# Six of eight GLU projection chunks as seven block products, with convolution steps moved to later stages, in a one-core decoder layer

## The chip, the cores and the metric

The kernel runs on one core of one Trainium2 chip. The metric is the device time of one execution in microseconds (us). Engines are named as in the profile: PE (TensorE, matmuls), PEld (its weight loads), DVE (VectorE), ACT (ScalarE), POOL (GpSimd), SP (SyncE, which here only issues transfers). PEq, ACTq, POOLq and SPq are the queues of instructions that issue DMAs.

## The reference, cut to what matters

One decoder layer for 512 prompt tokens and 8 sample tokens (520 rows together), width 1024:

```
xn   = rmsnorm(x);  proj = xn @ w_in
a_b, a_c, a_x, b_val, b_glu, q, gate_logits = split(proj)
ya = (a_b * dwconv3(a_c * a_x)) @ w_out_a
ub = b_val * sigmoid(b_glu)                                  # the GLU
yb = silu(layernorm(dwconv31(ub) + bias)) @ w_out_b          # 31 taps, depthwise, causal
yx = softmax(q k^T / 16) v @ w_out_x
h  = x + (g0 * ya + g1 * yb + g2 * yx) @ w_o;  h = h + SwiGLU(rmsnorm(h));  rmsnorm(h)
```

The change touches how `b_val` and `b_glu` (each 1024 columns of `xn @ w_in`) are multiplied, and when the 31 taps of `dwconv31` are computed. Outputs stay those of the reference.

## The kernel before

**Tiling.** Activations lie transposed: 8 tiles of 128 channels by 520 tokens (`TOK`; `HALF` is 260). A projection is done in chunks of 256 output columns over all 1024 input channels: a chunk is 1 MB of weights and two output tiles of 128 channels, each of which takes both 1 KB halves of one PSUM buffer (`acc`, four of them, used in turn; `free(use)` makes PE wait until the use four back was read, through the counter `acc_read`).

**Precision.** Each float32 operand is split in a high part (rounded by an ACT copy) and a low part (difference). A product is high x high + high x low + low x high: for a chunk 2 tiles x 8 input tiles x 2 halves x 3 = 96 matmuls of 128x128 by 260 columns, 64 with the high weights and 32 with the low (`chunk`, L2218 and L2236).

**Weights.** SP loads a chunk into one of two raw slots; ACT makes the high part (`hi_part`, L749) and mostly a negated copy (`negative`, L752), onto which POOL issues an accumulating DMA that adds the raw weights, which leaves the low part (L727; PE waits on `w_rest`). For the chunks listed in `SUB` (chunk 9, the second of the GLU stage, is the last before the convolution stages) POOL subtracts itself, two TENSOR_TENSOR of 128x1024 (L723).

**Stages**, in PE's order: keys and values; GLU (chunks 8 to 15: even chunks give gates, odd ones values; two chunks are a pair); queries and attention (Q, four heads); the products of the width-3 convolution (CX); branch X (gate and output chunks in turns, four pairs, on DVE in a loop of two); BA; branch A (four pairs); layer norm, branch B; w_o; feed-forward (FFN). All engines have one fixed order, written out by hand. DVE fills time between its stage duties with taps of the width-31 convolution: `conv` (L1462), 8 tiles x 32 steps (31 taps and one small step for the samples), each step dependent on the last. Before the change 62 steps lie in the GLU stage, 34 in Q, 32 in CX, 64 in X, 32 in BA and 32 in A.

**Seven block products.** Most FFN chunks already go as one level of Strassen-Winograd over 2x2 blocks: the 1024x256 weights and the 1024x520 activations are each cut in four, seven products of 512x128 by 512x260 replace eight, each of 12 matmuls, so 84 in place of 96 (`seven`, L2544 and L2551). DVE must make four sums of weight blocks, their low parts, and combine the products (7 adds of 260 columns); ACT makes the high parts and copies the first product out of PSUM after the third.

**Opening and end of the GLU stage.** DVE's last work before it is L1437 and L1441 (clearing of the convolution's padding); its first product of gates and values comes at the end of the first pair (L1487, which reads PSUM and frees it). ACT loads keys of the sample group (`load_k`, 1 MB each) in this stage, and splits the first Q chunk at its end.

Of the kernel before, what the change touches and what calls it, by code (L numbers as in the profile page):

```python
# [58 lines left out]
PARTS = ((0, 4), (4, 6), (10, 4), (14, 8))  # L59
PAIRS = HK  # L60
SEVEN = 8


def ffn_order():
# [150 lines left out]
def decoder_step(nc, x_prompt, x_sample, mem_prompt, cache_mem_k, cache_mem_v, state_conv_a,  # L215
# [109 lines left out]
    ln_sum = at("ln_sum", [P, TOK], f32, o_p2l)  # L325
    uao = at("uao", [TS + 2, D], f32, o_p2h)

    hg = [at(f"hg_{n}", [P, KT, TOK], f32r, o_ub + 4 * ACTV * i) for i, n in enumerate("hl")]
    y_st = at("y_st", [P, 4, D], f32, o_xh)
    ys_st = at("ys_st", [TS, D], f32, o_xh + 16 * D)  # L330
# [57 lines left out]
    with ctx:  # L388
# [38 lines left out]
        state_sum = sem("state_sum")  # L427
        pads = sem("pads")
        b_sig = sem("b_sig")
        ubo_stored = sem("ubo_stored")  # L430
        q_hi = sem("q_hi")
        q_rep = sem("q_rep")
# [130 lines left out]
        def ob(n):  # L563
            return T[f"ob{n // 2}"] + n % 2

        z_tmp = [ubyb[:, KT, 0:TOK], sg[:, 0, 0:TOK]]

        def kept(c, rows):
# [15 lines left out]
        def _(sp):  # L584
            def load(c, slot, src, col, k0=0, kn=KT):

                if not isinstance(c, int):
                    sp.wait_ge(w_own, own(c) - 4)
                elif c - 2 >= OWN:
                    sp.wait_ge(w_own, own(c - 2))  # L590
                elif c - 2 in SUB:
                    sp.wait_ge(w_sub, subtracted(c - 2))
                elif c >= 2:
                    sp.wait_ge(w_rest[slot], turn(c - 2) * 16)
                sp.dma_start(w_raw[:, slot, 0:kn, :], src[:, k0:k0 + kn, bass.ds(col, CW)]) \
                    .then_inc(w_loaded[slot], 16)

# [99 lines left out]
        def _(pool):  # L697
# [14 lines left out]
            for c in range(1, OWN):  # L712
                if c in SUB:
                    if c == 1:
                        pool.wait_ge(refined, 5)
                    if 2 <= c < C_B + 2:
                        pool.wait_ge(acc_done, T[f"kv{c - 2}"] + 1)
                    elif c >= C_B + 2:
                        pool.wait_ge(acc_done, T["c1" if c == C_CX + 2 else f"cx{c - C_CX - 2}"] + (1 if c == C_CX + 2 else 2))
                    for s in range(2):  # L720
                        ks = slice(s * HK, (s + 1) * HK)
                        pool.wait_ge(w_hi, 2 * c + s + 1)
                        nc.gpsimd.tensor_tensor(w_l[:, c % 2, ks, :], w_raw[:, c % 2, ks, :], f(w_h[:, c % 2, ks, :]),  # L723
                                                ALU.subtract).then_inc(w_sub, 1)
                else:
                    pool.wait_ge(w_neg, sum(n not in SUB for n in range(c + 1)))
                    pool.dma_start(w_l[:, c % 2, :, :].rearrange("p k n -> p (k n)"),  # L727
                                   w_raw[:, c % 2, :, :].rearrange("p k n -> p (k n)"),
                                   accum_op=ALU.add).then_inc(w_rest[c % 2], 16)
# [11 lines left out]
        def _(act):  # L741
# [138 lines left out]
            act.wait_ge(x_kept, 16 * 5)  # L880


            for p in range(4):
                u0 = T["b"] + 4 * p
                split(C_B + 2 * p + 1, 1, u0 - 1)
                for j in range(2):
                    done(u0 + j)

                    act.wait_ge(acc_read, u0)
                    nc.scalar.activation(two(sg[:, j, 2:SG]), halves(u0 + j), ACT.Sigmoid).then_inc(b_sig, 1)  # L890
# [365 lines left out]
        def _(dve):  # L1256
# [206 lines left out]
                    ins.then_inc(cv_step, 1)  # L1463

            CV = K_B + 1
            Q4 = (range(0, 12), range(12, 16), range(16, 28), range(28, CV))

            dve.wait_ge(pads, 1)  # L1470
            for i in range(2):
                for p in range(2):
                    u0 = T["b"] + 8 * i + 4 * p
                    if i + p:
                        dve.wait_ge(acc_read, T["b"] + 4)
                    if i == 0 and p == 1:
                        conv(0, range(20))
                    elif i and p == 0:
                        conv(0, range(20, K_B))
                        conv(1, range(9))  # L1480
                    elif i:
                        conv(1, range(9, 29))
                    dve.wait_ge(b_sig, 4 * i + 2 * p + 2)
                    for j in range(2):
                        n = 4 * i + 2 * p + j
                        done(u0 + 2 + j)
                        V.tensor_tensor(two(ubyb[:, n + 1, PAD:SLOT]), halves(u0 + 2 + j), two(sg[:, j, 2:SG]),  # L1487
                                        ALU.mult).then_inc(acc_read, 1 if j else 3)

            conv(1, range(29, K_B))  # L1490


            dve.wait_ge(acc_read, T["b"] + 16)
# [62 lines left out]
            taps = (0, 14, 19, 24, 29)  # L1556
            for h in range(NH):
                if h == 0:
                    conv(2, range(0, 3))
                q_lo(h, 0)  # L1560
                if h:
                    probs_lo(h - 1)
                conv(2, range(taps[h], taps[h] + 3) if h else range(3, 8))
                q_lo(h, 1)
                if h == 0:
                    done(T["btail"])
                    V.tensor_copy(ubo[:, :].rearrange("p (b c) -> p b c", b=2),
                                  acc[T["btail"] % 4][0:PAD + TS, :, :]).then_inc(acc_read, 1)
                    conv(0, [K_B])
                    conv(1, [K_B])  # L1570
# [5 lines left out]
                conv(2, range(taps[h] + 3, taps[h + 1]) if h else range(8, 11))  # L1576
                normalise(h, 1)
                if h:
                    sample_scores(h - 1, 1)
                if h == 0:  # L1580
                    conv(2, range(11, taps[1]))
            dve.wait_ge(c_copied, 1)
            probs_lo(3, 2)
            sample_scores(3, 0)
# [6 lines left out]
            conv(2, range(taps[NH], CV - 1))  # L1591

            conv(2, [K_B])

            def group_max():

# [65 lines left out]
            for it in range(4):  # L1662
# [11 lines left out]
                    group_max()  # L1674
                if it == 3:
                    sample_lo(0)
                conv(3, C3[it][0])
# [5 lines left out]
                for j in range(2):  # L1683
# [13 lines left out]
                conv(3, C3[it][1])  # L1697
                if it < 2:
                    sample_sum(it)
            sample_norm(2)  # L1700
# [1 line left out]
            sample_norm(3)  # L1702
            sample_lo(2)
            sample_lo(3)
            conv(3, range(24, CV))


            with dve.Fori(0, 2) as i:
                for p in range(2):
                    u0 = i * 8 + (T["x"] + 4 * p)  # L1710
                    conv(i + 4, Q4[2 * p])
                    dve.wait_ge(x_sig, i * 4 + (2 * p + 2))
                    for j in range(2):
                        done(u0 + (2 + j))
                        dst = merged_f[:, bass.ds(i * (4 * TOK) + (2 * p + j) * TOK, TOK)]
                        V.tensor_tensor(two(dst), halves(T["x"] + 4 * p + 2 + j), two(sg[:, j, 2:SG]),
                                        ALU.mult).then_inc(acc_read, 1 if j else 3)
                        if j == 0:
                            conv(i + 4, Q4[2 * p + 1])


            def ba_lo_part(n):
# [16 lines left out]

            dve.wait_ge(cs_step, KT - 1)  # L1740
            dve.wait_ge(cv_step, (KT - 1) * K_B)
            for k in range(1, KT - 1):
                V.tensor_tensor(ln_sum[:, :], ubyb[:, k, 0:TOK], ubyb[:, 0, 0:TOK] if k == 1 else ln_sum[:, :],
                                ALU.add).then_inc(ln_step, 1)
                dve.wait_ge(ln_step, k)


            for it in range(4):
                u0 = T["a"] + 4 * it
                if it < 3:  # L1750
                    conv(KT - 1, (range(0, 11), range(11, 22), range(22, CV))[it])
                else:
                    dve.wait_ge(cs_step, KT)
                    dve.wait_ge(cv_step, KT * K_B)
# [425 lines left out]
        def _(pe):  # L2180
# [195 lines left out]
            def q_tile(h, j):  # L2376
# [345 lines left out]
```

## Time and profile before

| | |
|---|---|
| Median of 3 runs | 1069.52 us (1069.45 to 1069.84) |
| The profiled execution's own time | 1069.33 us |
| Its span, first to last instruction | 1067.6 us (1.7 us of its time lie around the span) |
| Mean granted TensorE clock | 0.997 of full |
| DVE, ACT, POOL busy | 718.2, 479.7, 110.8 us |
| DMA, mean | 175 GB/s |

In timelines a row is: start in us from the span's start, duration in us, engine, line, operation, output<-inputs, shape, count, and in brackets the idle time before it with what ended it. A matmul's recorded duration (0.28 us) overlaps those of its neighbours; the distance between starts is what counts. Some matmul records can be missing.

### The profile page before, as it was taken

Reading aid. Unit: us, or ns where it says so; the run is one execution under the profiler, and the core shown is the slowest. Engines: PE = TensorE matmul, PEld = TensorE weight load, DVE = VectorE, ACT = ScalarE, POOL = GpSimd, SP = SyncE. Lnnn points to the kernel's source line nnn. Section 1 sums busy time; section 2 is a strip of 40 time slices with the busy share of each in tenths; the row PEclk is TensorE's granted clock in tenths of the full one; section 3 lists DMA queues with packets and bytes.
Section 4 is the critical chain, followed back from the end, with each engine's and each line's share of the span. In section 5 each row is a group of like instructions: output and inputs, shape, how many; then the busy total and the mean of one; then the engine's idle time right before and its main releaser. Section 6 shows DMA issues by size and latency. Waiting matters only on the chain.

```text
span 1067.6 us, 20526 instructions
## 1 busy us (share of the span) xinstructions
PE 1057.3 (99%) x8751; PEld 1051.1 (98%) x8751; DVE 718.2 (67%) x1234; ACT 479.7 (45%) x550; POOL 110.8 (10%) x93
## 2 busy tenths in 40 slices
PE   9999999999999999999999999999999999999997
PEld 9999999999999999999999999999999999999996
DVE  6766677888888654686323755578778457588754
ACT  6744443453335353344345723344456245366431
POOL 3661000002300000000000000000000000000000
PEclk9999999999999999999999999999999999999998
DMA  8967886689796878758876663231578365487512
GB/s 293 289 189 190 222 208 154 195 228 316 215 274 140 208 172 195 177 148 192 207 187 158 160 237 116 81 99 40 152 185 198 114 148 145 119 199 176 169 41 80
DMA packets 151194, 187.25 MB, mean 175 GB/s; under 512 B 4759, under 2 KB 141295, under 8 KB 145591
## 3 DMA queue, kind: packets, MB, share of 16 engines
q1 hardware_dynamic: 117734, 106.64, 31.8%
q0 software_dynamic: 8496, 57.15, 26.7%
q10 hardware_dynamic: 24880, 22.26, 6.9%
q8 instruction: 63, 1.03, 0.4%
q14 instruction: 21, 0.16, 0.1%
HBM read 122.34 MB, written 7.54 MB: 122 GB/s over the span
## 4 chain that ended last, share of the span: by engine, by line
PE 96%; DVE 3%; ACT 0%; issue 0%; POOL 0%; DVEq 0%; POOLq 0%
PE acc L2218 39%; PE acc L2236 20%; PE acc L2592 12%; PE acc L2544 11%; PE acc L2551 6%; PE acc L2329 2%; PE acc L2190 2%; PE acc L2337 1%; PE acc L2433 1%; PE acc L2409 1%; DVE o_acc L1631 0%; DVE ubyb L1462 0%; DVE yA L1693 0%; PE acc L2494 0%; DVE w_l L1337 0%
## 5 line engine op out<-in xcount | busy, mean ns | idle before, releaser
L2218 PE MATMUL acc<-big_h,w_h 128*128 128x260 f32 x1664 | 337.2, 284 | 0.1
L2218 PE MATMUL acc<-big_l,w_h 128*128 128x260 f32 x1664 | 334.4, 282 | 0.0
L2218 PEld LDWEIGHTS acc<-big_h,w_h 128*128 128x128 f32 x1664 | 255.8, 188 | 0.7 <-DVE st L1667 0.3
L2218 PEld LDWEIGHTS acc<-big_l,w_h 128*128 128x128 f32 x1664 | 256.4, 189 | 0.0
L2236 PE MATMUL acc<-big_h,w_l 128*128 128x260 f32 x1664 | 209.0, 283 | 0.0
L2236 PEld LDWEIGHTS acc<-big_h,w_l 128*128 128x128 f32 x1664 | 203.7, 189 | 0.1
L1462 DVE SCALAR_TENSOR_TENSOR ubyb<-ubyb,prm 128x512 f32<-128x512 f32 (+1 forms) x240 | 180.3, 751 | 15.1 <-DVE ubyb L1462 9.4
L749 ACT ACTIVATE w_h<-w_raw 128x1024 fp32r<-128x1024 f32 x120 | 120.2, 1051 | 103.5 <-DMA w_raw<-in_w_out_a_dram 29.7
L2544 PE MATMUL acc<-x_h,ws_h 128*128 128x260 f32 x504 | 126.0, 282 | 0.0
L2544 PE MATMUL acc<-x_l,ws_h 128*128 128x260 f32 x504 | 125.8, 282 | 0.0
L2544 PEld LDWEIGHTS acc<-x_h,ws_h 128*128 128x128 f32 x504 | 94.9, 188 | 0.2
L2544 PEld LDWEIGHTS acc<-x_l,ws_h 128*128 128x128 f32 x504 | 94.9, 188 | 0.0
L752 ACT ACTIVATE w_l<-w_raw 128x2048 fp32r<-128x2048 f32 x41 | 78.2, 1908 | 12.7 <-PE acc L2236 12.7
L727 POOL DMA_DIRECT2D w_l<-w_raw x41 | 35.1, 856 | 464.6 <-ACT w_l L752 464.6
L2551 PE MATMUL acc<-x_h,ws_l 128*128 128x260 f32 x504 | 81.2, 283 | 0.0
L2592 PE MATMUL acc<-mid,wd_h 128*128 128x260 f32 x576 | 72.6, 283 | 0.0
L2592 PEld LDWEIGHTS acc<-mid,wd_h 128*128 128x128 f32 x576 | 70.6, 189 | 0.0
L2551 PEld LDWEIGHTS acc<-x_h,ws_l 128*128 128x128 f32 x504 | 69.0, 188 | 0.0
L723 POOL TENSOR_TENSOR w_l<-w_raw,w_h 128x1024 fp32r<-128x1024 f32 x22 | 59.1, 2712 | 45.6 <-ACT w_h L749 32.3
L733 POOL DMA_DIRECT2D ws_l<-w_raw x18 | 15.3, 848 | 368.3 <-ACT ws_l L1168 368.3
L1168 ACT ACTIVATE ws_l<-w_raw 128x1536 fp32r<-128x1536 f32 x18 | 26.8, 1491 | 57.4 <-PE acc L2551 23.0
L1976 DVE TENSOR_TENSOR ws_f<-w_raw 128x1024 f32<-128x1024 f32 x18 | 22.0, 1223 | 32.9 <-PE acc L2592 15.9
(278 smaller groups left out, 1327.8 us busy)
## 6 DMA issues: line engine op xcount, KB each, us to landing
w_l<-w_raw POOLq DMA_DIRECT2D x41, 1024.0 KB, 8.1
w_raw<-in_w_in_dram SPq DMA_DIRECT2D x36, 1024.0 KB, 5.3
ws_l<-w_raw POOLq DMA_DIRECT2D x18, 768.0 KB, 7.4
w_raw<-in_w_ff_gate_dram SPq DMA_DIRECT2D x18, 512.0 KB, 5.0
w_raw<-in_w_ff_up_dram SPq DMA_DIRECT2D x18, 512.0 KB, 4.9
k_st<-in_cache_mem_k_dram ACTq DMA_DIRECT2D x8, 1024.0 KB, 8.2
v_st<-in_cache_mem_v_dram ACTq DMA_DIRECT2D x8, 1024.0 KB, 12.6
w_raw<-in_w_v_dram SPq DMA_DIRECT2D x4, 1024.0 KB, 8.0
```

What stands on the lines that cost most here:

```text
L723: nc.gpsimd.tensor_tensor(w_l[:, c % 2, ks, :], w_raw[:, c % 2, ks, :], f(w_h[:, c % 2, ks, :]), ALU.subtract).then_inc(w_sub, 1)
L727: pool.dma_start(w_l[:, c % 2, :, :].rearrange("p k n -> p (k n)"), w_raw[:, c % 2, :, :].rearrange("p k n -> p (k n)"), accum_op=ALU.add) ...
L749: nc.scalar.activation(w_h[:, slot, ks, :], w_raw[:, slot, ks, :], ACT.Copy).then_inc(w_hi, 1)
L752: nc.scalar.activation(w_l[:, slot, :, :], w_raw[:, slot, :, :], ACT.Copy, scale=-1.0).then_inc(w_neg, 1)
L1168: nc.scalar.activation(ws_l[s % 2][:, 0:3, :, :].rearrange("p b r n -> p (b r n)"), raw_f[:, s % 2, 1:4, :].rearrange("p b n -> p (b n)"), ...
L1462: ins = V.scalar_tensor_tensor(y, u, w, y, ALU.mult, ALU.add)
L1976: V.tensor_tensor(x[:, 3:5, :], raw_f[:, s % 2, 0:1, :].broadcast_to([P, 2, PAIRS * P]), raw_f[:, s % 2, 1:3, :], ALU.add).then_inc(st_sum, 1)
L2218: last = M.matmul(out[:, b, 0:HALF], w_h[:, slot, k, cols], xs[:, k_at + k, b * HALF:(b + 1) * HALF], start=start and k == 0 and xs is x[0 ...
L2236: last = M.matmul(out[:, b, 0:HALF], w_l[:, slot, k, cols], x[0][:, k_at + k, b * HALF:(b + 1) * HALF], start=False, stop=stop and k == ks ...
L2544: M.matmul(out, ws_h[slot][:, w, r, :], x_part[:, r, x, :], start=r == 0 and x_part is x_h, stop=False)
L2551: last = M.matmul(out, ws_l[slot][:, w, r, :], x_h[:, r, x, :], start=False, stop=r == PAIRS - 1)
L2592: last = M.matmul(out[:, b, 0:e - a], w, inner(kind[1], k, a, e), start=begin and k == ks[0] and kind is kinds[0], stop=end and k == ks[-1 ...
```

## The change

Chunks 10 to 15 of the GLU stage (`GLU_SEVEN = range(2, 8)`, j = 2 to 7) are computed by `glu_seven`, 84 matmuls each, in the same order of products as in the FFN. For them the weights are loaded as two DMAs of 512-byte rows; POOL's accumulating DMA covers three of four blocks. The four block combinations of `xn` are made once, by DVE (`xn_f` = high + low part again, then t1 to t4, then their low parts) and ACT (high parts), while PE does chunks 0 and 1. Results are left in quarters of `sg` (gates) and `ubyb` (values), which also hold the first product and its sums. The first `load_k` pair moves behind the split of the second Q chunk, as the region is now in use. Convolution steps per stage become 15 (GLU), 32 (Q), 32 (CX), 92 (X, unrolled), 40 (BA), 45 (A); the sum over the first seven tiles for the layer norm moves behind the first 13 steps of A. The core of the diff:

```diff
+GLU_SEVEN = range(2, 8)
@@ sync, load()
+                if isinstance(c, int) and c - C_B in GLU_SEVEN:
+                    for half, b, landed_ in ((1, 0, w_half), (0, 2, w_loaded)):
+                        sp.dma_start(raw_f[:, slot, b:b + 2, :]..., src[:, :, col + half * P:...]).then_inc(landed_[slot], 16)
+                    return
@@ scalar
-            for p in range(4):
-                split(C_B + 2 * p + 1, 1, u0 - 1)
-                for j in range(2): ... Sigmoid
-                split(C_B + 2 * p + 2, 0, u0 + 1)
-                if p >= 2:
-                    load_k(0, p - 2)
+            split(C_B + 1, 1, T["b"] - 1)
+            for n in range(4):
+                turned_hi(n)
+            for j in range(1, 8):
+                n, e = j + 1, j - 1
+                if j == 1:
+                    for i in range(2):
+                        done(T["b"] + i)
+                        nc.scalar.activation(two(sg[:, i, 2:SG]), halves(T["b"] + i), ACT.Sigmoid).then_inc(b_sig, 1)
+                if n < 8:
+                    glu_negative(n)
+                if j >= 2:
+                    glu_copy(j)          # waits for the third product of chunk j
+                if n < 8:
+                    glu_hi_sums(n, 0)
+                    glu_hi_sums(n, 1)
+                    glu_hi_raw(n)
+                else:
+                    split(C_Q, 0, T["b"] + 13)
+                if e % 2 == 0 and e:
+                    act.wait_ge(acc_read, T["b"] + 2 * e + 2)
+                    nc.scalar.activation(sg[:, :, 2:SG], sg[:, :, 2:SG], ACT.Sigmoid).then_inc(b_sig, 1)
...
+                if h == 0:
+                    for u in range(2):
+                        load_k(0, u)
@@ vector
+            a_, b_ = xn_f[:, 0:PAIRS, :], xn_f[:, PAIRS:KT, :]
+            dve.wait_ge(nrm_lo, 5)
+            for ks in (slice(0, PAIRS), slice(PAIRS, KT)):
+                V.tensor_tensor(xn_f[:, ks, :], f(xn[0][:, ks, :]), f(xn[1][:, ks, :]), ALU.add).then_inc(t_step, 1)
+            ...
+            V.tensor_tensor(t1, a_[:, :, early], a_[:, :, late], ALU.subtract).then_inc(t_step, 1)
+            V.tensor_tensor(t2, b_[:, :, late], t1, ALU.add).then_inc(t_step, 1)
+            V.tensor_tensor(t3, a_[:, :, late], b_[:, :, late], ALU.subtract).then_inc(t_step, 1)
+            V.tensor_tensor(t4, b_[:, :, early], t2, ALU.subtract).then_inc(t_step, 1)
...
+            for n in range(4):
+                turned_lo(n)
+            for j in range(1, 8):
+                n, e = j + 1, j - 1
+                if e == 1:
+                    dve.wait_ge(b_sig, 2)
+                    for i in range(2):
+                        done(T["b"] + 2 + i)
+                        V.tensor_tensor(two(ubyb[:, i + 1, PAD:SLOT]), halves(T["b"] + 2 + i), two(sg[:, i, 2:SG]),
+                                        ALU.mult).then_inc(acc_read, 1 if i else 3)
+                elif e > 1:
+                    glu_combine(e)       # five adds of 260 columns
+                    if e % 2:
+                        glu_product(e)
+                if n < 8:
+                    glu_sums(n, 0)
+                if j >= 2:
+                    glu_first(j)         # two adds of 260, behind glu_copy
+                if n < 8:
+                    glu_sums(n, 1)
+                    glu_low(n, 0)
+                    glu_low(n, 1)
+                if j >= 2:
+                    taps((2, 2, 0, 2, 0, 7)[j - 2])
+            glu_combine(7)
+            glu_product(7)
+            taps(2)
...
-            with dve.Fori(0, 2) as i:
-                for p in range(2):
-                    conv(i + 4, Q4[2 * p]) ... product ... conv(i + 4, Q4[2 * p + 1]) ... product
+            for p in range(4):
+                taps(17)
+                dve.wait_ge(x_sig, 2 * p + 2)
+                for j in range(2):
+                    done(u0 + 2 + j)
+                    V.tensor_tensor(two(merged[:, 2 * p + j, :]), ..., ALU.mult).then_inc(acc_read, 1 if j else 3)
+                    if j == 0:
+                        taps(6)
...
-                conv(6, range(4 * n, 4 * n + 4))
+                taps(5)
...
+                    else:
+                        taps((KT - 1) * CV - made)
+                        sum_first_tiles()
@@ tensor
+            def glu_seven(j):
+                free(u)
+                free(u + 1)
+                for n, (out, w, x) in enumerate(((Y, s1, t1), (X, s2, t2), (P_, a11, b11), (Z, a22, t4), (P_, a12, b21),
+                                                 (X, s3, t3), (Y, s4, b22))):
+                    ...      # waits: b_hi, b_lo (n < 2); w_hi, w_rest (n == 2); b_copy (4); b_uv (5, 6)
             for j in range(8):
-                chunk(C_B + j, j % 2, T["b"] + 2 * j, T["b"] + 2 * j, xn)
+                if j not in GLU_SEVEN:
+                    chunk(C_B + j, j % 2, T["b"] + 2 * j, T["b"] + 2 * j, xn)
+                    continue
+                if j == GLU_SEVEN[0]:
+                    pe.wait_ge(t_lo, 4)
+                glu_seven(j)
```

## Rows read from the trace of the kernel before

**Rows 1.** The page, part 1: busy us, share of the span, instructions.
```profile
PE 1057.3 (99%) x8751; PEld 1051.1 (98%) x8751; DVE 718.2 (67%) x1234; ACT 479.7 (45%) x550; POOL 110.8 (10%) x93
```

**Rows 2.** Waits of PE, whole span, longest first: us, times, longest.
```profile
PE acc L2190 <- POOL ident L703: 1.6, 1, 1.6
```

**Rows 3.** Timeline of DVE, GLU stage: second products of two pairs.
```profile
89.14 0.70 DVE L1487 TENSOR_TENSOR ubyb<-acc,sg 128x520 f32<-128x520 f32 x1 [1.11 <-PE acc L2236]
...
112.12 0.70 DVE L1487 TENSOR_TENSOR ubyb<-acc,sg 128x520 f32<-128x520 f32 x1 [1.11 <-PE acc L2236]
```

**Rows 4.** Timeline of DVE, FFN: first work behind two successive seven-product chunks.
```profile
829.13 0.43 DVE L2010 TENSOR_TENSOR cp<-acc,cp 128x260 f32<-128x260 f32 x1 [2.16 <-PE acc L2551]
...
839.17 0.43 DVE L2010 TENSOR_TENSOR cp<-acc,cp 128x260 f32<-128x260 f32 x1 [0.39 <-PE acc L2551]
```

**Rows 5.** Groups of DVE instructions in the FFN: count, busy us, mean ns, idle before.
```profile
L1988 DVE TENSOR_TENSOR ws_l<-ws_f,ws_h 128x1024 fp32r<-128x1024 f32 x36 | 42.3, 1217 | 0.0
L1979 DVE TENSOR_TENSOR ws_f<-ws_f,w_raw 128x512 f32<-128x512 f32 x18 | 12.5, 693 | 0.6
L2025 DVE TENSOR_TENSOR up_f<-up_f,gs 128x1040 f32<-128x1040 f32 x9 | 11.1, 1233 | 0.1
```

**Rows 6.** Timeline of DVE, before the GLU stage and in CX.
```profile
57.54 2.79 DVE L1313 TENSOR_TENSOR big_l<-nrm_o,big_h 128x1024 fp32r<-128x1024 f32 x1
...
71.93 0.26 DVE L1441 MEMSET ubyb<- 128x240 f32 x1
...
267.58 5.63 DVE L1631 SCALAR_TENSOR_TENSOR o_acc<-v_st,pT,o_acc 128x256 f32<-128x256 f32 x14
```

**Rows 7.** Timeline of PE: start of the third GLU chunk.
```profile
88.93 0.40 PE L2218 MATMUL acc<-big_h,w_h 128*128 128x260 f32 x2
```

**Rows 8.** Timeline of POOL, GLU stage and CX.
```profile
72.91 4.74 POOL L723 TENSOR_TENSOR w_l<-w_raw,w_h 128x1024 fp32r<-128x1024 f32 x2 [5.10 <-ACT w_h L749]
...
105.22 0.84 POOL L727 DMA_DIRECT2D w_l<-w_raw  x1 [13.00 <-ACT w_l L752]
...
151.20 0.84 POOL L727 DMA_DIRECT2D w_l<-w_raw  x1 [13.03 <-ACT w_l L752]
...
269.59 8.41 POOL L723 TENSOR_TENSOR w_l<-w_raw,w_h 128x1024 fp32r<-128x1024 f32 x2 [6.46 <-ACT w_h L749]
```

**Rows 9.** Timeline of SP: weight loads that waited for those POOL transfers.
```profile
112.19 0.37 SPq L595 DMA_DIRECT2D w_raw<-in_w_in_dram  x1
...
160.34 12.66 SPq L595 DMA_DIRECT2D w_raw<-in_w_in_dram  x2
```

**Rows 10.** Timeline of ACT: the split of the first Q chunk.
```profile
147.10 2.00 ACT L749 ACTIVATE w_h<-w_raw 128x1024 fp32r<-128x1024 f32 x2
149.00 1.91 ACT L752 ACTIVATE w_l<-w_raw 128x2048 fp32r<-128x2048 f32 x1
```

**Rows 11.** Timeline of DVE: end of CX, and branch X.
```profile
332.44 5.47 DVE L1462 SCALAR_TENSOR_TENSOR ubyb<-ubyb,prm 128x512 f32<-128x512 f32 x7
...
371.88 0.70 DVE L1716 TENSOR_TENSOR merged<-acc,sg 128x520 f32 x1 [7.04 <-PE acc L2236]
```

**Rows 12.** Timeline of DVE: end of BA, start of branch A.
```profile
472.29 1.20 DVE L1736 COPY uao<-acc 10x1024 f32<-10x1024 f32 x1
...
474.13 3.64 DVE L1743 TENSOR_TENSOR ln_sum<-ubyb,ln_sum 128x520 f32<-128x520 f32 x5
...
487.83 0.70 DVE L1760 TENSOR_TENSOR sg<-acc,sg 128x520 f32<-128x520 f32 x1 [1.59 <-PE acc L2236]
488.64 0.70 DVE L1763 TENSOR_TENSOR merged<-merged,sg 128x520 f32<-128x520 f32 x1
```

**Rows 13.** Window at the end: length, busy PE, PEld, DVE, ACT, POOL, PEclk, DMA, GB/s.
```profile
1060.00:1064.00 4.00, 0.65 (x8) 0.54 (x8) 3.45 (x11) 1.54 (x3) 0.00 (x0) 0.72 0.12 46
```

**Rows 14.** Timeline of PE, first microseconds of the span.
```profile
1.59 3.67 PE L2190 MATMUL acc<-ident 128*128 128x128 f32 x16 [1.59 <-POOL ident L703]
...
8.40 0.82 PE L2190 MATMUL acc<-ident 128*128 128x128 f32 x6
```

More of the change, by code:

```diff
@@ L880, in _, with turned_hi @@
             act.wait_ge(x_kept, 16 * 5)
-            for p in range(4):
-                u0 = T["b"] + 4 * p
-                split(C_B + 2 * p + 1, 1, u0 - 1)
[L886 to L890, printed above, removed]
-                split(C_B + 2 * p + 2, 0, u0 + 1)
-                if p >= 2:
-                    load_k(0, p - 2)
+            def turned_hi(n):
+                act.wait_ge(t_step, 2 + n + 1)
+                nc.scalar.activation(tx[0][:, n, :, :].rearrange("p r t -> p (r t)"), tx_f[:, n, :], ACT.Copy).then_inc(t_hi, 1)
@@ new lines, in glu_first, with combs @@
+            def glu_first(j):
+                u, k = T["b"] + 2 * j, j - 2
+                m1, v, u2, _ = glu_quarters(j)
+                dve.wait_ge(b_copy, k + 1)
+                V.tensor_tensor(u2, m1, acc[u % 4][:, 1, 0:HALF], ALU.subtract).then_inc(b_uv, 1)
+                dve.wait_ge(b_uv, 2 * k + 1)
+                V.tensor_tensor(v, acc[(u + 1) % 4][:, 0, 0:HALF], u2, ALU.add).then_inc(b_uv, 1)
+            def combs(j):
+                return sum(5 if n % 2 else 4 for n in range(2, j))
@@ new lines, in glu_combine @@
+            def glu_combine(j):
+                u, k = T["b"] + 2 * j, j - 2
+                c11, c12, c21, c22 = glu_quarters(j)
+                P_, X, Y, Z = (acc[(u + n // 2) % 4][:, n % 2, 0:HALF] for n in range(4))
+                dve.wait_ge(b_uv, 2 * k + 2)
+                done(u + 1)
+                V.tensor_tensor(c22, X, c12, ALU.subtract).then_inc(b_comb, 1)
+                V.tensor_tensor(c21, X, c21, ALU.subtract).then_inc(b_comb, 1)
+                V.tensor_tensor(c11, P_, c11, ALU.add).then_inc(b_comb, 1)
+                dve.wait_ge(b_comb, combs(j) + 1)
+                V.tensor_tensor(c12, Y, c12, ALU.add).then_inc(b_comb, 1)
+                dve.wait_ge(b_comb, combs(j) + 2)
+                ins = V.tensor_tensor(c21, Z, c21, ALU.add)
+                ins.then_inc(*((b_comb, 1) if j % 2 else (acc_read, 2)))
@@ L1562, in _ @@
                     probs_lo(h - 1)
-                conv(2, range(taps[h], taps[h] + 3) if h else range(3, 8))
+                taps(3 if h else 5)
                 q_lo(h, 1)
@@ L1575, in _ @@
                 query_rows(h)
-                conv(2, range(taps[h] + 3, taps[h + 1]) if h else range(8, 11))
+                taps(q_taps[h + 1] - q_taps[h] - 3 if h else 3)
                 normalise(h, 1)
@@ L1580, in _ @@
                 if h == 0:
-                    conv(2, range(11, taps[1]))
+                    taps(3)
             dve.wait_ge(c_copied, 1)
@@ L1696, in _ @@
                         group_bias()
-                conv(3, C3[it][1])
+                taps(len(C3[it][1]))
                 if it < 2:
@@ L1704, in _ @@
             sample_lo(3)
-            conv(3, range(24, CV))
-            with dve.Fori(0, 2) as i:
[L1709 to L1719, printed above, removed]
+            taps(8)
+            for p in range(4):
+                u0 = T["x"] + 4 * p
+                taps(17)
+                dve.wait_ge(x_sig, 2 * p + 2)
+                for j in range(2):
+                    done(u0 + 2 + j)
+                    V.tensor_tensor(two(merged[:, 2 * p + j, :]), halves(u0 + 2 + j), two(sg[:, j, 2:SG]),
+                                    ALU.mult).then_inc(acc_read, 1 if j else 3)
+                    if j == 0:
+                        taps(6)
             def ba_lo_part(n):
@@ L1737, in _, with sum_first_tiles @@
                 .then_inc(acc_read, 1)
[L1740 to L1745, printed above, removed]
+            def sum_first_tiles():
+                dve.wait_ge(cs_step, KT - 1)
+                dve.wait_ge(cv_step, (KT - 1) * K_B)
+                for k in range(1, KT - 1):
+                    V.tensor_tensor(ln_sum[:, :], ubyb[:, k, 0:TOK], ubyb[:, 0, 0:TOK] if k == 1 else ln_sum[:, :],
+                                    ALU.add).then_inc(ln_step, 1)
+                    dve.wait_ge(ln_step, k)
             for it in range(4):
@@ L1750, in _ @@
                 if it < 3:
-                    conv(KT - 1, (range(0, 11), range(11, 22), range(22, CV))[it])
+                    if it:
+                        taps((KT * CV - made) // (3 - it))
+                    else:
+                        taps((KT - 1) * CV - made)
+                        sum_first_tiles()
                 else:
```

164 lines of the change are left out of this document (139 added, 25 removed).

## The prediction, made before the result was known

> **What bounds the kernel now.** I read the page's busy times first, then PE's waits, then the timelines of the GLU stage engine by engine, then the same of the FFN, where the new kind of chunk already runs. The page has PE busy 99% of the span [rows 1], and its longest wait in the whole span is 1.6 us, before any data is there [rows 2]; no other is over 0.5. So PE sets the time everywhere, and no stage has slack that would take up a new stall: a matmul saved is time saved, and a microsecond in which PE waits is a microsecond lost. The reader is to see both sides of that in what follows.
>
> **What PE saves.** The second products of two pairs lie 22.98 us apart, each with the same short wait for PE [rows 3], so a plain chunk takes 11.49 us for its 96 matmuls. Two successive seven-product chunks in the FFN end 10.04 us apart [rows 4], 84 matmuls at the same 0.120 us. The difference is 1.45 us, times six chunks: -8.7 us.
>
> **Inside the six chunks** I replayed DVE's and ACT's lists from the start S of a chunk. DVE on an odd j: combine from S+0.2 (five adds of 260 columns, 0.43 each by [rows 4], 0.34 apart where pipelined: 1.7), first weight sums 1.2, a wait for ACT's copy of the third product (3 x 12 x 0.120 = 4.3, done by S+4.9), two adds, to S+5.8, two sums of 512 (1.4), two low parts (2.4) [rows 5], two taps: free at S+11.0, 0.8 behind the next chunk's first duty. On an even j the product of gates and values (1.23, the 1040-element row of [rows 5]) takes the place of the taps: free at S+9.7 of a chunk of 10.04, so the lag is gone. PE's nearest demand, the second add before its seventh product, stands at S+8.6 against S+6.0. ACT ends at S+10.6 at worst. I put stalls here at 0; the bound above is the 0.8 lag at each of three pairs, 2.4 us.
>
> **The opening** is where cover is missing. PE may start chunk 10 only when DVE's product of the first pair has freed PSUM (`free`), and the new order puts that product behind everything DVE makes for the block products. DVE is free at 72.2, after the clearing of the padding [rows 6]. Its list: two sums of 2080 elements (1.233 us at 1040 against 0.693 at 512 is 1.02 ns an element [rows 5], so 2.3 each, 4.55), four of 1040 (4.8), their four low parts (4.65), the three weight sums (1.2 + 0.7 + 0.7), two low parts of 1024 (2.35), the product itself (0.70, [rows 3]). Sum 19.7: 91.9. PE wants chunk 10 at 88.9 [rows 7]. That alone is a stall of 3.0.
>
> It is not alone. POOL's two subtractions for chunk 9 start at 72.91 and take 4.74 us [rows 8] while DVE is idle in the kernel before; now they fall on top of DVE's sums. A DVE instruction of two SBUF operands, 1024 elements, took 2.79 us at 57.54, while POOL ran the same kind of subtraction [rows 6], against 1.22 for that size in the FFN [rows 5]: they take turns, and the one waits for the other's whole instruction. DVE's new list has such instructions one upon the other, so both subtractions are inserted whole: +4.75, DVE reaches 96.6, and the opening stall is 7.7. ACT's four high parts, table load, sigmoids and the negation end near 91.2 and POOL's transfer lands by 98.7, before PE wants it at 100.4; they hide. From below the collision costs nothing, if POOL is the one held off.
>
> The Trainium skill (SBUF — State Buffer, on engine ports) says that DVE with two SBUF inputs and a GpSimd instruction that reads SBUF exclude each other, and that whoever issues first wins. DVE's first sum, at 72.2, is first. By the trace this can go on: at 269.59 two subtractions took 8.41 us, as DVE's 14 back-to-back instructions at 0.40 us each lost nothing meanwhile [rows 6, 8]. By that reading DVE would lose nothing until a gap; but five of the new instructions wait for the one before, and a gap is all that POOL needs, so I stay with 4.75.
>
> **The clock.** A PE idle for 7.7 us may come back slower. In the last 4 us with matmuls the granted clock averages 0.72 [rows 13]: between its two levels, 2.4 and 1.2 GHz (1.00 and 0.50), that is 1.8 us at the upper, though PE was busy for 0.65 us only; it fell about 1.1 us after the last matmul. In the opening 16 transposes took 3.67 us, 0.23 each, and 6 later ones 0.82, 0.11 apart [rows 14]: half speed for about 5.4 us after the first matmul. If that recurs, 5.4 us at half speed lose 2.4 to 2.7; I take 2.5, from 0 to 2.7. The skill (TensorE: Matmul & The Clock Gate, Part 1) agrees in kind: throttled is the default, and activity lifts it.
>
> **The end of the GLU stage.** The first Q chunk's split now stands behind ACT's copy in chunk 15: with S7 the start of that chunk, copy to S7+4.8, two high parts 2.0, negation 1.9 [rows 10], POOL's transfer at S7+8.9. From POOL's issue to the load that waits for its landing is 7.0 us where no other transfer runs (105.22 to 112.19) and 9.1 where one of the key loads does (151.20 to 160.34) [rows 8, 9]. The key loads are now issued at about S7+13.7, so I take 7.0 and a little: landing at S7+16.0. PE asks for that low part 32 matmuls into the first Q tile, at S7+10.04+3.83 = 13.9. Stall 2.2 (2.0 to 4.1 by the two rows). Before, the landing was at 160.3 against a demand at 161.7.
>
> **The moved steps.** A tap is 0.785 us (7 in 5.47, [rows 11]). 47 fewer in the GLU stage pay for the new sums. In X each pair gets 17 + 6. Inside the stage DVE needs 23 x 0.785 + 1.4 = 19.5 of 22.98 us and keeps up, the more so as the unrolled steps lose some 0.15 us each of loop arithmetic. But at its start DVE comes straight from CX: 8 steps from 332.4, then 16 and the small one, ends at 351.5. The product is due at 371.88 - 22.98 = 348.9 [rows 11] and frees the PSUM that PE needs 1.6 us later, at 350.5 (at 88.93 PE began the next chunk [rows 7], and the first product of that pair had begun 1.11 + 0.70 ahead of 89.14 [rows 3], at 87.3); it now frees it at 352.25. Stall 1.75 (0 to 2.6).
> BA: 5 taps and two operations of 520 elements (0.70 each) are at most 5.35 of the 48 x 0.120 = 5.75 us of a tile; it keeps up, but ends later: the copy at 472.29 [rows 12] moves to 474.4, two more taps and the exchange of a small step for a tap. Then 12 taps and a small step (9.7), and only then the 4.3 us of sums that used to come first (473.5 to 477.8): 489.7, where the first product of A is due at 487.83 and was released with its merge at 489.34, just ahead of PE [rows 12]. Stall 1.7 (0 to 2.2). In CX the exchange of a small step for a tap costs at most 0.1.
>
> **The sum**, against the profiled execution: 1069.33 - 8.7 + 7.7 + 2.5 + 2.2 + 1.75 + 1.7 + 0.1 = 1076.6, which stands 7.1 us above the median before, 0.7%. The profiled execution is 0.2 below the median of the runs shown, which is nothing beside this. Other edits are taken at nothing: the two half loads of 512-byte rows (the FFN's chunks have the same and keep 10.04), the keys, which land during the first head and are read in the second, and the unrolled loop.
>
> **The rivals.**
> R1, no slower clock: everything else as above, 1074.1. For it: that the clock fell so soon at the end may be due to the thin work ahead of it, and here PE comes out of a dense stretch. Against: 7.7 us is long beside 1.1.
> R2, no collision with POOL: DVE goes on undisturbed, the opening stall is 3.0 and the clock holds: 1069.33 - 8.7 + 3.0 + 5.75 = 1069.4, no change. For it: the 14 undelayed instructions. Against: the 2.79 us one, and there are others of 2.3 to 2.9 like it.
> R3, the other side: the opening list fits. It decides at the product's place: if DVE's sums of 2080 elements and POOL's turns together cost no more than lets the product end by 88.9 to 89.7 (a list of 17 us or less, not 24.4), the first stall vanishes, and 1069.33 - 8.7 + 5.75 = 1066.4; with the X and A stalls gone as well 1062.9. For it: each of these durations is read from another place. Against: it needs 3 us less than the sum without any collision.
> R4, the chunks don't keep their 10.04: DVE's lag isn't worked off (for a collision with POOL's descriptor work, say), 2.4 us or more on top: 1079 and up.
>
> **How the numbers follow.** The forecast 0.42, R1 0.22, R2 0.10, R3 0.10, R4 0.16. A measurement of this kernel can tell about 0.2%, 2.1 us, from no change. Forecast, R1 and R4 are slower beyond that, 0.78 with small parts of R1 lost to no change; R2 falls within; R3 is faster. So slower 0.78, same 0.11, faster 0.11. For 8 in 10 I leave out R3 and the tail of R4: 1069.2 to 1080.5; the likeliest case by itself spans 1074.5 to 1078.5.
>
> **What would show it.** In the trace after: PE idle 7 to 8 us before the third GLU chunk, near 96.6, released by DVE's product; DVE's sums of 2080 and 1040 elements and POOL's subtractions stretched, 4.7 us between them; a granted clock below 1 right after; then six chunk ends 10.04 apart; a wait of PE on the w_l transfer of 2 us in the first Q tile; waits on DVE of 1.5 to 2 us at the second gate chunk of X and of A. It is wrong if PE starts chunk 10 before 93, if the chunks are further apart than 10.1, or if the total of PE's new waits is under 10 us.

## The result, and the profile after

The changed kernel takes 1087.11 us (median of 4, 1083.71 to 1087.76) beside 1069.68 for the one before in the same session (4, 1069.45 to 1070.41): a ratio of 1.0155 (ratios here and below are of the means), 95% interval 1.0134 to 1.0177; by the medians it is 17.4 us slower. The forecast was 1076.6, slower by 7.1, and its range ended at 1080.5. The profiled executions are 1087.76 and 1069.33, the spans 1086.0 and 1067.6. The ledger below goes by the spans, +18.4.

The page after (busy us, share of the span, instructions), beside [rows 1]: 72 matmuls fewer, PE's busy time 1.6 us less, and yet the span is longer: PE now stands still, where it did not before. DVE has 64 us more work.

```profile
PE 1055.7 (97%) x8679; PEld 1048.3 (97%) x8679; DVE 782.1 (72%) x1313; ACT 491.8 (45%) x563; POOL 111.1 (10%) x93
```

PE's waits after, by whom they were for, beside [rows 2] (us in total, times, longest). The largest total stands on a transfer, not on DVE:

```profile
PE acc L2432 <- DMA w_l<-w_raw: 8.2, 2, 4.7
PE acc L2600 <- DVE ubyb L1666: 7.9, 1, 7.9
PE acc L2414 <- DVE merged L1906: 1.6, 1, 1.6
PE acc L2386 <- POOL ident L746: 1.6, 1, 1.6
PE acc L2790 <- ACT cp L1284: 1.0, 2, 0.6
```

DVE's timeline after, in the opening (start, us, instruction), where [rows 6] had only the clearing of the padding. Two sums of 2080 elements took 6.76 us together (2.33 and 4.52 one by one, overlapping by 0.1), the next two, of 1040, took 3.33 and 1.24; the product, two halves, is the last but one line:

```profile
73.11 0.26 DVE L1537 MEMSET ubyb<- 128x240 f32 x1
73.41 6.76 DVE L1577 TENSOR_TENSOR xn_f<-big_h,big_l 128x2080 f32<-128x2080 f32 x2
80.20 3.33 DVE L1580 TENSOR_TENSOR tx_f<-xn_f 128x1040 f32<-128x1040 f32 x1
83.57 1.24 DVE L1582 TENSOR_TENSOR tx_f<-xn_f,tx_f 128x1040 f32<-128x1040 f32 x1
...
96.76 1.30 DVE L1666 TENSOR_TENSOR ubyb<-acc,sg 128x520 f32<-128x520 f32 x2
97.98 1.22 DVE L1604 TENSOR_TENSOR sw_f<-w_raw 128x1024 f32<-128x1024 f32 x1
```

POOL's timeline after, which answers to [rows 8]: its two subtractions took 8.34 us (3.90 and 4.48 one by one) for 4.74. The last two lines are the transfers of which the waits below speak.

```profile
74.09 8.34 POOL L766 TENSOR_TENSOR w_l<-w_raw,w_h 128x1024 fp32r<-128x1024 f32 x2 [3.96 <-ACT w_h L797]
...
159.66 0.84 POOL L775 DMA_DIRECT2D w_l<-w_raw  x1 [15.92 <-ACT w_l L800]
...
492.96 0.86 POOL L775 DMA_DIRECT2D w_l<-w_raw  x1 [18.03 <-ACT w_l L800]
```

PE's timeline after at the three long waits; the second line, the start of chunk 10, answers to [rows 7]. The matmuls beside each wait are the measure of the clock: 16 with the low part took 3.84 us at 169.53 and 2.09 at 177.93, 32 took 5.61 at 501.42 and 4.00 at 85.79.

```profile
85.79 4.00 PE L2432 MATMUL acc<-big_h,w_l 128*128 128x260 f32 x32
97.72 0.56 PE L2600 MATMUL acc<-tx_h,sw_h 128*128 128x260 f32 x1 [7.92 <-DVE ubyb L1666]
...
169.53 3.84 PE L2432 MATMUL acc<-big_h,w_l 128*128 128x260 f32 x16 [4.72 <-DMA w_l<-w_raw]
...
177.93 2.09 PE L2432 MATMUL acc<-big_h,w_l 128*128 128x260 f32 x16
...
501.42 5.61 PE L2432 MATMUL acc<-big_h,w_l 128*128 128x260 f32 x32 [3.48 <-DMA w_l<-w_raw]
```

Windows after around them (the clock is the third number from the end): 2.4 GHz before the first wait, 1.2 GHz behind all three. In the first and second the clock fell while PE still waited. In the third it fell about 1.5 us after PE had started again: that was at 501.42, and the window to 503 still has 0.98.

```profile
85.00:89.00 4.00, 4.00 (x36) 4.00 (x35) 3.96 (x4) 3.83 (x4) 0.00 (x0) 1.00 0.66 178
89.00:95.00 6.00, 0.79 (x7) 0.59 (x5) 5.90 (x7) 4.59 (x6) 1.00 (x1) 0.86 0.25 49
95.00:100.00 5.00, 2.29 (x10) 2.32 (x11) 4.20 (x5) 3.27 (x3) 0.86 (x1) 0.50 0.61 126
169.00:175.00 6.00, 5.47 (x25) 5.47 (x26) 0.89 (x3) 0.60 (x1) 0.00 (x0) 0.50 1.07 256
501.00:503.00 2.00, 1.58 (x13) 1.58 (x14) 0.87 (x2) 0.00 (x0) 0.00 (x0) 0.98 1.05 201
503.00:506.00 3.00, 3.00 (x15) 3.00 (x15) 1.40 (x2) 0.00 (x0) 0.00 (x0) 0.50 0.85 136
```

And ACT's copies of the third product of the seven-product chunks; the first and the last of six are 50.33 us apart, 10.07 each:

```profile
104.94 0.39 ACT L962 ACTIVATE sg<-acc 128x260 f32<-128x260 f32 x1 [6.67 <-PE acc L2608]
115.00 0.39 ACT L962 ACTIVATE ubyb<-acc 128x260 f32<-128x260 f32 x1 [2.74 <-PE acc L2608]
...
155.27 0.39 ACT L962 ACTIVATE ubyb<-acc 128x260 f32<-128x260 f32 x1 [4.84 <-PE acc L2608]
```

**The ledger of the spans** (waits by their brackets). PE comes to the opening 0.7 us later than before: its 32 matmuls with the low part of chunk 9 start at 85.79 for 85.10, ahead of all that was changed. The six chunks give back 8.5. The opening stall costs 7.9 and the clock behind it 2.7: the first 36 matmuls of chunk 10 took 7.0 us, where 0.120 each make 4.3. The first Q tile costs 4.7, and its clock 2.6: from 169.53 on, 26 matmuls took 5.76 us where 0.120 each make 3.12. X costs 1.6. A costs 3.5, and its clock 1.6 in 32 matmuls. In the FFN, PE waits 1.0 us for ACT's copy. The sum is 17.8. The other 0.6 is in the waits: counted between the starts of matmuls, each is 0.1 to 0.2 us longer than in its bracket.

### The profile page after: what moved, and what is told of

Same layout as the page of the kernel before. It is cut to its first block, busy times and chain, and to the rows that moved or that the text cites. A ratio compares the mean times of both kernels' runs of the same rounds, so it can differ in the third digit from the quotient of the medians.

```text
span 1086.0 us, 20360 instructions
## 1 busy us (share of the span) xinstructions
PE 1055.7 (97%) x8679; PEld 1048.3 (97%) x8679; DVE 782.1 (72%) x1313; ACT 491.8 (45%) x563; POOL 111.1 (10%) x93
## 4 chain that ended last, share of the span: by engine, by line
PE 59%; DVE 4%; DMA 4%; ACT 1%; issue 0%; ACTq 0%; SPq 0%; DVEq 0%
PE acc L2414 23%; PE acc L2432 12%; PE acc L2838 11%; PE acc L2790 9%; PE acc L2797 5%; DVE ubyb L1558 2%; DMA ws_l<-w_raw 1%; DMA w_raw<-in_w_ff_gate_dram 1%; DMA w_raw<-in_w_ff_up_dram 1%; DMA w_l<-w_raw 1%; PE acc L2386 0%; ACT ws_l L1264 0%; PE acc L2740 0%; DVE ws_f L2172 0%; ACT ws_h L1272 0%
## 5 line engine op out<-in xcount | busy, mean ns | idle before, releaser
L2414 PE MATMUL acc<-big_h,w_h 128*128 128x260 f32 x1472 | 298.5, 284 | 1.7 <-DVE merged L1906 1.6
L2414 PE MATMUL acc<-big_l,w_h 128*128 128x260 f32 x1472 | 296.1, 283 | 0.0
L2414 PEld LDWEIGHTS acc<-big_h,w_h 128*128 128x128 f32 x1472 | 227.0, 189 | 2.5 <-issue 1.8
L2414 PEld LDWEIGHTS acc<-big_l,w_h 128*128 128x128 f32 x1472 | 227.1, 189 | 0.0
L2432 PE MATMUL acc<-big_h,w_l 128*128 128x260 f32 x1472 | 188.2, 285 | 8.2 <-DMA w_l<-w_raw 8.2
L2432 PEld LDWEIGHTS acc<-big_h,w_l 128*128 128x128 f32 x1472 | 183.3, 191 | 8.6 <-DMA w_l<-w_raw 8.6
L1558 DVE SCALAR_TENSOR_TENSOR ubyb<-ubyb,prm 128x512 f32<-128x512 f32 x240 | 180.3, 751 | 7.3
L797 ACT ACTIVATE w_h<-w_raw 128x1024 fp32r<-128x1024 f32 x108 | 108.2, 1052 | 90.0 <-DMA w_raw<-in_w_in_dram 24.7
L775 POOL DMA_DIRECT2D w_l<-w_raw x35 | 29.9, 855 | 422.7 <-ACT w_l L800 422.7
L800 ACT ACTIVATE w_l<-w_raw 128x2048 fp32r<-128x2048 f32 x35 | 66.8, 1908 | 8.6 <-PE acc L2432 8.6
```

The costliest lines, as they stand in the source:

```text
L797: nc.scalar.activation(w_h[:, slot, ks, :], w_raw[:, slot, ks, :], ACT.Copy).then_inc(w_hi, 1)
L800: nc.scalar.activation(w_l[:, slot, :, :], w_raw[:, slot, :, :], ACT.Copy, scale=-1.0).then_inc(w_neg, 1)
L1558: ins = V.scalar_tensor_tensor(y, u, w, y, ALU.mult, ALU.add)
L2414: last = M.matmul(out[:, b, 0:HALF], w_h[:, slot, k, cols], xs[:, k_at + k, b * HALF:(b + 1) * HALF], start=start and k == 0 and xs is x[0 ...
L2432: last = M.matmul(out[:, b, 0:HALF], w_l[:, slot, k, cols], x[0][:, k_at + k, b * HALF:(b + 1) * HALF], start=False, stop=stop and k == ks ...
```

## The experiments

Four kernels on one chip, beside 1070.34 us for the kernel before (7 runs); then three on another, beside 1071.09 (15 runs). The kernel before was thus 0.7 and 1.4 us slower there than in the session above, by whose times the expectations go.

**Without the collision in the opening.** Chunk 9's low part comes from ACT's negation and POOL's transfer; the subtraction is gone.

```
-SUB = (*range(C_B + 2), C_CX + 2, C_CX + 4)
+SUB = (*range(C_B + 1), C_CX + 2, C_CX + 4)
```

> The changed kernel, with the low part of chunk 9 made by ACT's negated copy and an accumulating transfer, so that GpSimd subtracts nothing in the opening of the GLU stage. Theory (collision plus clock): DVE's two sums of 2080 elements take 2.3 us each again, its list ends 4.7 us earlier, the wait of PE before the third chunk falls from 7.9 to about 3.2 us, and the clock stays at its upper level there, which gives back another 2.8: 7.5 us less than the changed kernel, about 1079.5. Rival (DVE's list is long by itself, GpSimd only fills gaps in it): the wait stays at 7 or more and the time at 1087. A third way, the collision goes but the clock falls all the same: 4.7 less, 1082.4.

Measured: 1081.02 us (1078.06 to 1082.84), 1.0097 of before (1.0071 to 1.0123). Its DVE timeline has the undisturbed durations, and its PE timeline a wait of 3.05 us:

```profile
71.92 4.56 DVE L1577 TENSOR_TENSOR xn_f<-big_h,big_l 128x2080 f32<-128x2080 f32 x2
76.52 1.24 DVE L1580 TENSOR_TENSOR tx_f<-xn_f 128x1040 f32<-128x1040 f32 x1
```

```profile
91.94 0.36 PE L2600 MATMUL acc<-tx_h,sw_h 128*128 128x260 f32 x1 [3.05 <-DVE ubyb L1666]
...
92.97 0.74 PE L2608 MATMUL acc<-tx_h,sw_l 128*128 128x260 f32 x4
...
95.25 1.07 PE L2608 MATMUL acc<-tx_h,sw_l 128*128 128x260 f32 x4
...
97.39 0.64 PE L2608 MATMUL acc<-big_h,w_l 128*128 128x260 f32 x4
```

The collision was worth 2.2 + 2.1 us in two instructions, 4.3 where 4.75 was forecast. The stall fell by 4.9; the other 0.6 is that DVE began its list 1.5 us earlier than after, and PE came to the stall only 0.9 earlier. The clock fell all the same, after 1.5 us of matmuls at full speed: four took 0.74 us at 92.97, 1.07 at 95.25 and 0.64 at 97.39. So a stall of 3 us in place of 7.9 did not save the clock, but the fall cost less: the first 36 matmuls took 5.93 us, 1.6 too many, against 2.7 after.

**The Q chunk's split ahead of the copy.**

```
                 if n < 8:
                     glu_negative(n)
+                if n == 8:
+                    split(C_Q, 0, T["b"] + 13)
                 if j >= 2:
                     glu_copy(j)
...
-                else:
-                    split(C_Q, 0, T["b"] + 13)
```

> The changed kernel, with the split of the first Q chunk ahead of ACT's copy of the first product in chunk 15 instead of behind it. Theory (the split stands too late): the transfer is issued about 4.4 us earlier, near S7+4.4, lands near S7+12 with nothing beside it, before PE's demand at S7+13.9; the wait of 4.7 us and the 2.5 us at the lower clock behind it both go, 7.2 us less than the changed kernel, about 1079.9. Rival (the transfer is slow because the transfer engines are full of other traffic, not because of its start): it still lands late and no more than 4.4 us come back.

Measured: 1078.72 us (1077.42 to 1079.92), 1.0078 (1.0061 to 1.0095). POOL issues the transfer at 153.11 for 159.66 (1.3 of this is only that chunk 10 starts earlier in this profiled execution, at 96.37 for 97.72), PE's waits on low parts are one where they were two, and the clock holds in Q (waits of PE, POOL's timeline, a window, of this kernel). The wait that is left, 3.2, is A's:

```profile
PE acc L2432 <- DMA w_l<-w_raw: 3.2, 1, 3.2
```

```profile
153.11 0.84 POOL L775 DMA_DIRECT2D w_l<-w_raw  x1 [10.90 <-ACT w_l L800]
```

```profile
160.00:180.00 20.00, 19.32 (x161) 18.79 (x160) 17.26 (x29) 8.02 (x16) 0.86 (x1) 1.00 0.93 270
```

The median is 8.4 us below the change's: the wait (4.7) and its clock (2.6) make 7.3. The rest is within the spread of the runs; in this kernel's profiled execution the clock also held in A.

**The keys' loads behind the first Q tile.**

```
+                q_part(h, 0)
                 if h == 0:
                     for u in range(2):
                         load_k(0, u)
-                q_part(h, 0)
```

> The changed kernel, with the two loads of keys (1 MB each) issued behind ACT's first Q copy instead of ahead of it; the split stands where it did. Theory (keys delay the low part): the transfer for the first Q chunk takes 7.0 to 7.5 us from issue to landing in place of 9.9, PE's wait falls from 4.7 to about 2.1 us, and at 2.1 us the clock may hold: 2.6 us less, or 5.1 with the clock, 1082 to 1084.5. Rival (keys are no part of it): the transfer takes 9.9 again and nothing changes.

Measured: 1084.42 us (1083.51 to 1086.24), 1.0133 (1.0116 to 1.0151). The key loads go out at 169.42 in place of 161.03. POOL's issue at 157.81 is as late in its chunk as after, but the wait is 2.74 for 4.72: the transfer lands 7.9 us behind its issue (157.81 to 165.71), not 9.9 (159.66 to 169.53). The clock fell behind this shorter wait too (3.66 us for 16 matmuls), though for a shorter time:

```profile
165.71 3.66 PE L2432 MATMUL acc<-big_h,w_l 128*128 128x260 f32 x16 [2.74 <-DMA w_l<-w_raw]
```

So 2.0 of the stall's 4.7 are the two key loads beside the transfer; the rest, near the forecast's 2.2, is the late split.

**ACT's wait for the conv tail behind the gates of A.**

```
+            gate_stage(T["a"], C_A, R_BG + BR_A, a_sig)
             act.wait_ge(acc_read, T["ctail"] + 1)
             act.dma_start(conv_a_prompt[0, 0], uao[0:2, :]).then_inc(uao_stored, 16)
             act.dma_start(conv_a_sample[0, :, 1, :], uao[2:2 + TS, :]).then_inc(uao_stored, 16)
-            gate_stage(T["a"], C_A, R_BG + BR_A, a_sig)
```

> The changed kernel, with ACT's wait for DVE's copy of the width-3 convolution's tails, and the two small stores behind it, moved from ahead of branch A's gate stage to behind it. Theory (ACT is held up by the copy that DVE now makes 2 us later, so the low part of the first output chunk of A starts late): PE's wait of 3.5 us on that transfer goes, and the 1.5 us at the lower clock with it; what is left is the wait on DVE's first product of A that was predicted, 1.7 us: 3.3 us less, about 1083.8. Rival (the transfer itself is late for want of bandwidth): the wait on the transfer stays above 2 us.

Measured: 1084.43 us (1080.7 to 1085.37), 1.0116 (1.0093 to 1.0139). POOL's issue stands at 486.61 in place of 492.96, the wait on the transfer is gone, and the wait on DVE that the forecast had put here (1.7) comes out from under it, 1.79:

```profile
503.75 0.50 PE L2414 MATMUL acc<-big_h,w_h 128*128 128x260 f32 x2 [1.79 <-DVE merged L1959]
```

What ACT stood behind in the changed kernel is DVE's late copy:

```profile
486.71 1.20 DVE L1926 COPY uao<-acc 10x1024 f32<-10x1024 f32 x1
```

```profile
488.85 2.01 ACT L797 ACTIVATE w_h<-w_raw 128x1024 fp32r<-128x1024 f32 x2 [6.42 <-DVE uao L1926]
490.77 1.90 ACT L800 ACTIVATE w_l<-w_raw 128x2048 fp32r<-128x2048 f32 x1
```

**The moved steps alone**, in the kernel before; all GLU chunks stay plain.

```
+            def taps(count):
+                nonlocal made
+                for step_ in range(made, made + count):
+                    conv(step_ // CV, [step_ % CV])
+                made += count
...
-                    if i == 0 and p == 1:
-                        conv(0, range(20))
...
+                    if i + p:
+                        taps(5)
```

The stages Q, CX, X, BA and A then call `taps` as in the change.

> The kernel before, all eight GLU chunks plain, with nothing but the convolution steps moved as in the change (15 in the GLU stage, the unrolled 92 in X, 40 in BA, 45 in A, and the sums of seven tiles behind the first 13 steps of A). Theory (the moved steps cost by themselves, at two places, and nowhere in the GLU stage): a wait of PE of 1.6 us in the first pair of X and of 3.5 us on the low part of the first output chunk of A, 1 to 1.5 us more where the clock falls behind the second: 1069.5 + 6.3, 1074.5 to 1076.5. Rival (these waits only come about through the new phase of the transfers behind the block products): under 2 us, 1069 to 1071.

Measured: 1075.65 us (1074.75 to 1076.09), 1.0046 (1.003 to 1.0061): 4.6 above before, not the 6.3 expected. The total lies in the expected range only because the kernel before was slower on this chip (1071.09, not 1069.5). PE's waits and the two low parts of A:

```profile
PE acc L2236 <- DMA w_l<-w_raw: 2.0, 1, 2.0
PE acc L2218 <- DVE merged L1710: 1.6, 1, 1.6
```

```profile
490.81 4.10 PE L2236 MATMUL acc<-big_h,w_l 128*128 128x260 f32 x32 [2.04 <-DMA w_l<-w_raw]
```

The two waits exist without any seven-product chunk, so they are the moved steps' own. Here A's is 2.0, not 3.5, with the clock held (4.10 for 32); POOL's issue was at 483.80 and the landing 7.0 us later, against 8.5 in the changed kernel (492.96 to 501.42). What made that landing longer is open.

**Four mends at once:** the first, second and fourth edit above, and DVE's steps placed otherwise: three fewer ahead of the first product in X (and one more ahead of each later one), and in A the sums of the seven tiles one pair later.

```
-                taps(17)
+                taps(18 if p else 14)
...
-                    if it:
+                    if it == 0:
+                        taps((KT - 1) * CV - made)
+                    else:
+                        if it == 1:
+                            sum_first_tiles()
                         taps((KT * CV - made) // (3 - it))
-                    else:
-                        taps((KT - 1) * CV - made)
-                        sum_first_tiles()
```

> The changed kernel with the edits of the first three lists together: no subtraction by GpSimd in the opening, the Q split first, ACT's stores behind branch A's gates; and with 4 steps fewer ahead of the first pair's product in X (14 + 6, then 18 + 6), the sums of seven tiles one pair later in A. Theory: only the opening is left, 3.1 us and 1.6 at the lower clock, and about 1 in the FFN: 1069.5 - 8.5 + 5.7 = 1066.7. Rival (one stall removed lets the next come out, as the transfers are full): 1070 or more.

Measured: 1069.29 us (1065.97 to 1070.02, 10 runs), 0.9977 (0.9968 to 0.9986). The waits of Q, X and A are gone; the longest left is the opening's 3.62. That is 2.6 above the expectation's 1066.7, of which 1.6 is the slower kernel before. The opening stall was 3.6 for 3.1, with 2.4 by the clock behind it (36 matmuls in 6.69 us) for 1.6, and PE waited 1.7 us in the FFN for 1.

**And the first pair's product between the sums and low parts of chunk 10,** one half each side of the low parts' two instructions, in place of behind them (the old place is left out below).

```
                     glu_sums(n, 1)
+                    if j == 1:
+                        first_product(0)
                     glu_low(n, 0)
                     glu_low(n, 1)
+                    if j == 1:
+                        first_product(1)
```

> The kernel with the four mends, and DVE's first product of the first pair ahead of the two low parts of chunk 10 instead of behind them and of the second sums. Theory (PE waits for that product alone, not for the low parts, which it asks for 1 and 2.4 us later): the opening wait falls from 3.1 to at most 1 us, no clock is lost, 1069.5 - 8.5 + 2 = 1063. Rival (the low parts are as late as the product): the wait moves to them and 1 us at most comes back.

Measured: 1064.55 us (1062.86 to 1065.13, 5 runs), 0.9942 (0.9929 to 0.9956). It beats both kernels: 6.5 us below the one before, 4.7 below the last; the expected 1063 is met once the same 1.6 are added. PE's start of the third chunk, with a wait of 0.46, and a window over it:

```profile
89.31 0.36 PE L2606 MATMUL acc<-tx_h,sw_h 128*128 128x260 f32 x1 [0.46 <-DVE ubyb L1662]
```

```profile
80.00:90.00 10.00, 9.54 (x80) 9.37 (x80) 9.90 (x10) 8.49 (x9) 0.86 (x1) 1.00 0.82 193
90.00:100.00 10.00, 10.00 (x86) 10.00 (x85) 8.60 (x12) 6.07 (x6) 0.84 (x1) 1.00 0.75 166
```

Against the last kernel the stall of 3.2 us and the half speed behind it are gone.

## Why the prediction came out too low

**What held.** The saving: 10.07 us a chunk for 11.49 [rows 3], no stall between the chunks; R4 is refuted. The opening: 7.9 for 7.7, behind DVE's product. That is in part luck, as two errors cancel: the collision was 4.3 for 4.75, and the list without it took 20.0 us (71.92 to 91.94 in the first experiment) for 19.7. DVE also reached its list 1.2 us later than in [rows 6], PE its stall only 0.7. R2 is refuted by the trace after, where both of POOL's subtractions stand between DVE's sums, and by the experiment without them. R3 is refuted by the latter too, since even then PE waited 3.05; its reasoning came true only in the last kernel, where the product was moved. The Trainium skill's exclusion of the two (SBUF — State Buffer, on engine ports) agrees with the trace: DVE's first sum started at 73.41, ahead of POOL at 74.09, and took its undisturbed 2.33; POOL's first subtraction was held off, 3.90 for 2.4; then DVE's second and third sum and POOL's second subtraction took 2.1 to 2.2 us more each. The reading that DVE, having issued first, would lose nothing does not hold: that was so for its first instruction only, and in all DVE lost 4.3 us, POOL 3.6. The clock in the opening: 2.7 for 2.5, so R1 is refuted. X: 1.6 for 1.75.

**What failed: three terms, 8.5 us of the 11.2 by which the span's change was missed (18.4 for 7.25).**
- *The end of the GLU stage*, put at 2.2, was 4.7. With S7, the start of chunk 15, at 150.76, POOL's issue came at S7+8.9 as forecast. The step "The key loads are now issued at about S7+13.7, so I take 7.0 and a little" failed: they were issued at 161.03, S7+10.3, beside the transfer. ACT's timeline shows why: the loads have the time 161.03, while the split of the next Q chunk, which stands ahead of them in the program, still computed until 164.4, S7+13.7. The 9.1 of [rows 8, 9], which the prediction had as its other end, was the right row, and 9.9 the measurement.

```profile
160.62 1.06 ACT L797 ACTIVATE w_h<-w_raw 128x1024 fp32r<-128x1024 f32 x1 [0.31 <-PE acc L2600]
161.03 3.18 ACTq L923 DMA_DIRECT2D k_st<-in_cache_mem_k_dram  x2
...
162.54 1.90 ACT L800 ACTIVATE w_l<-w_raw 128x2048 fp32r<-128x2048 f32 x1
```

- *The clock* was counted at one stall. It fell behind three: 2.6 more in Q and 1.6 in A, 4.2 together. The prediction asked the question of the long stall only.
- *The moved steps at A*: 1.7 was forecast for DVE's sums ahead of the gates. The size is right (1.79 when uncovered), but another waiter came first. That the copy at 472.29 moves by 2.1 us was worked out rightly (it lay 13.2 us ahead of PE's demand before, and 11.1 after), but who waits for that copy was not asked: ACT does, ahead of the split of A's first output chunk. In the kernel before, that chunk's low part had nothing in reserve: POOL issued its transfer at 478.53, and PE took it up at 485.55, 7.0 us later and 0.1 us after it could have. The stall of 3.5 is the 2.1 by which the issue moved, and a landing that took 8.5 us for 7.0; the wait on DVE lay inside it.

```profile
478.53 0.85 POOL L727 DMA_DIRECT2D w_l<-w_raw  x1 [15.85 <-ACT w_l L752]
```

```profile
485.55 4.09 PE L2236 MATMUL acc<-big_h,w_l 128*128 128x260 f32 x32
```

Another 1.7 are in no term. One part is the 0.7 ahead of the opening: in the stage of keys and values PE waited 0.8 us for a high part by ACT and 0.4 for a low part by POOL. Kernels with the same code there cleared the padding between 71.41 and 73.25, and the one with the moved steps alone, which has the code of the kernel before there, waited 1.1 us for ACT. That speaks for a spread of executions and against an effect of the change. The other part is 1.0 in the FFN. All seven kernels with the changed GLU stage have this wait (1.0 to 1.9 us), the two without it have none. ACT waits there 6.17 us for the gate weights' landing, and 5.52 before. Why the landing is later stays open. The last 1.0 is small differences of the other terms and the 0.6 of the ledger.

## What to carry to other kernels

When work is moved into an engine's queue, list who waits for each of its later results, small copies for an output too: in A the waiter that had been missed was a store's. A stall on the path is to be priced with the half-speed stretch behind it: in these kernels 2.7 us and more of waiting could bring 1.6 to 2.7 on top (and up to 3.3 us of it sometimes nothing). Before adding work to a stage, see whether the result that frees PSUM can go ahead of it: four mends of the waits turned a loss of 17.4 us into a gain of 1.8, and moving one product made that 6.5.

## What the runs showed of the hardware that was not expected

- The clock fell behind PE waits of 2.7, 3.05, 3.1, 3.5, 3.6 us and all longer ones, and held behind waits of 1.6, 1.8, 2.0, 3.2 and 3.3 (the last two in A, with the split first and without the subtraction: 4.10 us for the 32 matmuls in both). From 2.7 to 3.3 us it went either way; the length of the wait alone does not tell.
- The fall can come after the wait is over. Behind 3.05 us in the opening and behind 3.5 us in A, PE first ran about 1.5 us at full speed.
- DVE sums and POOL subtractions that met, all with two inputs in SBUF, took turns: 4.52 us for 2.3 and 3.33 for 1.24 on DVE, 3.90 and 4.48 for 2.4 on POOL.
- ACT issued a load 3.4 us before the compute that stands ahead of it in its program was done (161.03 against 164.4), and 0.4 us after its last wait was met.
- The accumulating transfer of a low part landed 7.9 us behind its issue with the key loads away, and 9.9 with them beside it.
